# Own tokens and keys transposed by DMAs, and the state pass on two pairs of PSUM banks

## The reference, cut to what matters

```python
xm = rmsnorm(x, norm_w) * (1.0 + sc_x) + sh_x            # modulation from c
parts_x, (qx, kx, vx) = split_heads(xm @ w_in, rotary=True)   # w_in: 1024 x 9216
s_f, s_b = ctx_final_states(kc, vc, lg[0], lg[1])        # from the context tokens
# retention, chunks of 128 positions, 8 heads, k 64 wide and v 128 wide, both directions:
scores = einsum('bhnid,bhnjd->bhnij', qc, kc) * dmask
inner = einsum('bhnij,bhnjv->bhniv', scores, vc)
kv = einsum('bhnjd,hj,bhnjv->bhndv', kc, k_dec, vc)      # each chunk's addition to the state
s = chunk_decay * s + kv                                 # chunk after chunk
cross = einsum('bhnid,hi,bhndv->bhniv', qc, q_dec, s_prev)
y_a = (silu(za) * bg * (dwconv(cg * h) + conv_b)) @ w_a  # the convolution branch
y_b = (silu(zb) * groupnorm(inner + cross)) @ w_b        # the retention branch
x = x + g_x * ((sigmoid(ga) * y_a + sigmoid(gb) * y_b) @ w_out)
out = rmsnorm(x, final_norm_w)
```

## Time and profile before

| | |
|---|---|
| time, median of 3 runs | 910.59 us (909.9 to 910.84) |
| the profiled execution, its own time | 909.72 us |
| its span on the slowest core (core 7) | 908.2 us |
| spans of the eight cores | 898.9 to 908.2 us |
| PE, DVE, ACT, POOL busy over the span | 90%, 49%, 40%, 35% |
| state pass, core 7 | 137.66 to about 251 us |

### The profile page before, as it was taken

One profiled execution on the slowest core, in us unless ns is written; L12 is line 12 of the kernel. 1 busy time (PEld: TensorE's weight loads), 2 busy tenths in 40 slices (PEclk: granted clock), 3 DMA queues, 4 the chain that ended last, 5 costly groups with the idle time before them and its releaser, 6 DMA issues.

```text
span 908.2 us, 14424 instructions; the slowest of 8 cores (898.9 to 908.2 us)
## 1 busy us (share of the span) xinstructions
PE 815.4 (90%) x4656; PEld 394.1 (43%) x4656; DVE 447.4 (49%) x1057; ACT 366.9 (40%) x653; POOL 318.5 (35%) x337
## 2 busy tenths in 40 slices
PE   0179999989975999998989999999999999999995
PEld 0145455545543444344444444444444444444442
DVE  3467515656766755666624424442364511343435
ACT  3499556677556434434323212222122211122122
POOL 0046325454567354444510123202242233233341
PEclk9999999989999899999999999999999999999998
DMA  8987603930074134132451362244006070034233
GB/s 245 292 258 189 158 12 100 179 113 7 10 115 96 32 48 48 33 51 52 71 91 25 64 123 41 53 93 93 1 1 139 27 160 0 23 107 150 72 115 139
DMA packets 49824, 82.33 MB, mean 91 GB/s; under 512 B 29259, under 2 KB 35531, under 8 KB 48086
## 3 DMA queue, kind: packets, MB, share of 16 engines
q1 hardware_dynamic: 44422, 54.14, 21.5%
q0 software_dynamic: 5328, 27.27, 17.0%
HBM read 93.72 MB, written 8.39 MB: 112 GB/s over the span
## 4 chain that ended last, share of the span: by engine, by line
PE 76%; DVE 7%; ACT 7%; DMA 5%; issue 3%; POOL 1%; SPq 1%; DVEq 0%; ACTq 0%; POOLq 0%
PE P L989 51%; PE P L560 12%; PE P L1253 6%; DMA wt<-ada_w 4%; ACT tm L967 2%; DVE vb L1004 2%; PE P L676 2%; PE P L456 1%; DVE tm L815 1%; DVE cm L941 1%; ACT st L892 1%; PE P L620 1%; PE P L933 1%; PE P L934 1%; PE P L801 1%
## 5 line engine op out<-in xcount | busy, mean ns | idle before, releaser
L989 PE MATMUL P<-xmt,vb 128*128 128x512 bf16 x1280 | 283.1, 379 | 2.7 <-DVE wt L1152 1.8
L989 PEld LDWEIGHTS P<-xmt,vb 128*128 128x128 bf16 x1280 | 124.5, 98 | 152.5 <-issue 3.6
L560 PE MATMUL P<-wt,xmt 128*128 128x512 bf16 x688 | 163.0, 389 | 5.7 <-ACT xmt L482 3.4
L989 PE MATMUL P<-xmt,wt 128*128 128x512 bf16 x512 | 118.3, 383 | 1.5 <-ACT tm L967 1.5
L560 PEld LDWEIGHTS P<-wt,xmt 128*128 128x128 bf16 x688 | 65.8, 100 | 84.3 <-issue 15.0
L1155 POOL TENSOR_TENSOR kz<-tm,wt 128x1024 bf16<-128x1024 f32 x16 | 45.7, 2857 | 161.3 <-DVE wt L1152 161.3
L989 PEld LDWEIGHTS P<-xmt,wt 128*128 128x128 bf16 x512 | 49.7, 99 | 59.3 <-issue 4.4
L1232 DVE SCALAR_TENSOR_TENSOR tm<-tm,P 128x512 f32<-128x512 f32 x32 | 22.0, 688 | 87.5 <-PE P L989 87.5
L989 PE MATMUL P<-vb,wt 128*128 128x512 bf16 x256 | 60.0, 387 | 5.5 <-DVE vb L1004 5.5
L1234 POOL TENSOR_TENSOR st<-st,tm 128x512 bf16<-128x512 bf16 x32 | 39.8, 1245 | 65.8 <-DVE tm L1232 65.8
L1108 DVE TENSOR_TENSOR wt<-P,wt 128x512 f32<-128x512 f32 x32 | 22.2, 693 | 80.9 <-ACT wt L1107 60.0
(11 more groups left out here) (163 smaller groups left out, 1109.7 us busy)
## 6 DMA issues: line engine op xcount, KB each, us to landing
kz<-x SPq DMA_DIRECT2D x24, 512.0 KB, 8.1
wt<-x SPq DMA_DIRECT2D x24, 512.0 KB, 4.3
vb<-w_conv POOLq DMA_DIRECT2D x16, 512.0 KB, 7.4
out<-wt SPq DMA_DIRECT2D x15, 512.0 KB, 3.6
st<-ada_w SPq DMA_DIRECT2D x2, 2048.0 KB, 13.9
wt<-ada_w SPq DMA_DIRECT2D x2, 2048.0 KB, 28.6
vb<-w_mix POOLq DMA_DIRECT2D x8, 512.0 KB, 8.7
cm<-rope SPq DMA_DIRECT2D x33, 64.0 KB, 3.2
```

The source lines that it names most:

```text
L560: ins = e.matmul(pf(bank)[:, 0:wid], lhsT=lhs_x(ch, k), rhs=w[:, k, c0_:c0_ + wid], start=(k == 0), stop=(k == 7))
L989: ins = e.matmul(pf(bank), lhsT=lhs(k), rhs=rhs(k), start=(k == 0), stop=(k == 7))
```

## The change

Four things change, all in the state pass or just ahead of it.

- **Own tokens.** `f_tp` is gone for own pairs. A new `f_dtp` lets SP transpose a chunk's scaled rows by one DMA from `xs` straight into `xm`, and `f_aff(pair, True)` modulates them there in place. The DMAs of a pair are issued at the end of the loop's pass in which it was scaled, one pair earlier than its PE transposes stood.
- **Keys.** `w2` has a DMA from SP in place of the PE transposes and ACT's copy; the rotated keys have four buffers in place of two.
- **States.** A chunk's two states go to banks 5 and 6 or to 7 and 0 in turn, its keys to bank 2 or 1. The state update and the copy are split by banks: DVE takes the first bank while ACT takes the second, then they change over.
- **Weights.** `w_q` comes in two parts of 0.5 MB, in the second and third pair, `w_zb` in four, in the fourth to seventh.

```diff
+        def f_dtp(pair):
+            for ch in pair:
+                blk, j = ch["xm"]
+                P.dma("sp", lambda e, ch=ch, blk=blk, j=j: e.dma_start_transpose(out=xm[blk][:, :, j * 128:(j + 1) * 128], in_=ch["xs"][0]),
+                      f"tx{ch['n'] % 4}", reads=[ch["xs"][1]], writes=[f"xm{blk}_{j}"])
...
-            P.op("dve", f_d, reads=["P0", "Amod", "modT"], writes=[n_ + "d" for n_ in names])
-            P.op("act", f_a, reads=["P1", "Amod", "modT"], writes=[n_ + "a" for n_ in names])
+            P.op("dve", f_d, reads=["Amod", "modT"] + (nd if inplace else ["P0"]), writes=nd)
+            P.op("act", f_a, reads=["Amod", "modT"] + (na if inplace else ["P1"]), writes=na)
...
-            proj(2, ch, wk, "wk")
+            kb = 2 if j else 1
+            proj(kb, ch, wk, "wk")
...
+            P.dma("sp", lambda e: e.dma_start_transpose(out=kT[:, n], in_=k_rb[n % 4].rearrange("p h f -> p (h f)")),
+                  f"tk{n % 4}", reads=[f"k_rb{n % 4}"], writes=[f"kT{n}"])
+            kv = (7, 0) if j else (5, 6)
...
+            def stf_half(q):
+                P.op("act", lambda e: e.activation(out=st[0:64, n + 1, q * 512:(q + 1) * 512], in_=pf(kv[q])[0:64, :], func=AF.Copy),
+                     reads=[f"P{kv[q]}"], writes=[f"stf{n + 1}_{q}"])
...
+                P.op("dve", f, reads=[f"P{kv[q]}", f"R{q}", "dec"], writes=[f"R{q}"])
+            for q in range(2):
+                if n > 0:
+                    state_half(q)
+                if n < 15:
+                    stf_half(1 - q)
...
-            if p == 1:
-                wload("wq", wq, wq_d)
-                wload("wzb", wzb, wzb_d)
+            if p in (1, 2):
+                k0 = 4 * (p - 1)
...
             w1(hi)
             if prev:
                 w2(prev)
             if p < 7:
-                f_tp(ownp[p + 1])
-                f_aff(ownp[p + 1])
+                f_aff(ownp[p + 1], True)
             w1(lo_)
             scale2(9 + p + 2)
             w2(hi)
+            if p < 6:
+                f_dtp(ownp[p + 2])
```

More of the change, by code:

```diff
@@ L220, in build_program @@
         own("R", TMP + 4096, 4096, "h")
+        for q in range(2):
+            own(f"R{q}", TMP + 4096 + q * 2048, 2048, "h")
         kc = at(TMP + 8192, [128, 8, 64], BF16)
@@ L223, in build_program @@
         own("kcs", TMP + 8192, 2048)
-        k_rb = [buf(f"k_rb{i}", TMP + 10240 + i * 1024, [128, 8, 64], BF16) for i in range(2)]
+        k_rb = [buf(f"k_rb{i}", TMP + 10240 + i * 1024 if i < 2 else EX + 6144 + (i - 2) * 1024, [128, 8, 64], BF16) for i in range(4)]
         kfb = [buf(f"kfb{i}", TMP + 12288 + i * 2048, [128, 8, 128], BF16) for i in range(2)]
@@ L255, in build_program @@
             own(f"stb{n}", ST + n * 2048, 2048, "h")
+            for q in range(2):
+                own(f"stf{n}_{q}", ST + n * 2048 + q * 1024, 1024, "l")
         mb = at(ST, [128, 4, 4096], BF16)
@@ L267, in build_program @@
             own(f"wv{k}", WB + k * 2048, 4096)
+        for k in (0, 4):
+            own(f"wq{k}", WQ + k * 1024, 4096)
+        for k in range(0, 8, 2):
+            own(f"wzb{k}", WZB + k * 2048, 4096)
         wk = buf("wk", WGB, [128, 8, 512], BF16)
@@ L648, in build_program @@
             scale2(p + 2)
+            if p == 7:
+                f_dtp(ownp[0])
             load2(p + 4)
@@ L719, in build_program @@
         scale2(10)
+        f_dtp(ownp[1])
         rope2(10)
@@ L800, in f_kv, with state_half, f @@
                 for h in range(8):
-                    ins = e.matmul(pf(5 + h // 4)[:, (h % 4) * 128:(h % 4 + 1) * 128], lhsT=kfb[j][:, h, :],
+                    ins = e.matmul(pf(kv[h // 4])[:, (h % 4) * 128:(h % 4 + 1) * 128], lhsT=kfb[j][:, h, :],
                                    rhs=vb[:, n, h * 128:(h + 1) * 128], start=True, stop=True)
                 return ins
[L804 to L811, removed]
+            P.op("pe", f_kv, reads=[f"kfb{j}", f"v{n}"], writes=[f"P{b}" for b in kv])
+            def stf_half(q):
+                P.op("act", lambda e: e.activation(out=st[0:64, n + 1, q * 512:(q + 1) * 512], in_=pf(kv[q])[0:64, :], func=AF.Copy),
+                     reads=[f"P{kv[q]}"], writes=[f"stf{n + 1}_{q}"])
+            def state_half(q):
+                def f(e):
                     ins = None
-                    for h in range(8):
-                        pk_ = pf(5 + h // 4)[:, (h % 4) * 128:(h % 4 + 1) * 128]
+                    for h in range(4 * q, 4 * q + 4):
+                        pk_ = pf(kv[q])[:, (h % 4) * 128:(h % 4 + 1) * 128]
                         ins = e.scalar_tensor_tensor(out=RF[64:128, h, :], in0=RF[64:128, h, :], scalar=dch[64:128, 8 + h:9 + h],
@@ L817, in f_state @@
                     return ins
-                P.op("dve", f_state, reads=["P5", "P6", "R", "dec"], writes=["R"])
+                P.op("dve", f, reads=[f"P{kv[q]}", f"R{q}", "dec"], writes=[f"R{q}"])
+            for q in range(2):
+                if n > 0:
+                    state_half(q)
+                if n < 15:
+                    stf_half(1 - q)
+            if n > 0:
                 put_stb(n - 1)
```

31 lines of the change are left out of this document (15 added, 16 removed).

## The result

The changed kernel takes **897.94 us** (median of four runs, 897.22 to 903.56) against 910.72 for the kernel before on the same chip: ratio 0.9878, 95% interval 0.9861 to 0.9896, so 1.2% faster. The forecast was 890.0, own range 885 to 893: the sign and most of the mechanism came, 8 us of the gain did not. The time lies outside that range, and inside 885 to 902, which was drawn to hold rivals (1) and (3) as well. The profiled execution took 897.38 us, its slowest core 895.7.

The account below looks back on a forecast made before the run. PE was taken to set the state pass's pace, so work and waits leaving its stream count. Slowest span 887.5 - 0.9 + 1.1 = 887.7, against 908.2; 889.2 for the profiled execution, 890 us as median, range 885 to 893.

Parts of the forecast that it names:

- rival (1): State pass: x rows come late behind transposes and weights, one or two stalls, 895 to 901, say 898 us; chance 0.17.
- rival (3): State pass: DVE's modulation from SBUF and POOL's products block each other, 0.4 to 1.5 six times, say 895 us; chance 0.12.
- PE's stream: First key projection to last state matmuls: 91.2 us of PE work remains, against 113.0 on core 7 and 108.0 on core 4.
- The 0.9 ahead: Ahead of the state pass: the eighth own pair's transposes leave PE's gapless work, another 0.9 us off.
- The state update: State pass: with two pairs of banks and halves crossing over, PE's wait for DVE's update costs nothing.
- The query wait: End of the state pass: PE waits 1.2 us at the first query transposes, against 0.16 before.
- +1.1: End of the state pass: the amount added to the sum for the new wait of 1.2 us against 0.16.
- The weights' stall: State pass: with weights in 0.5 MB parts, x arrives free by 1 us and the stall of 192 us goes.
- The modulation unchanged: State pass: modulating in place from SBUF takes as long as from PSUM, 1.3 us (DVE) and 1.8 (ACT) a pair.
- The cover: State pass pairs of 11.24 us: ACT, DVE and POOL work fits; own transposes landing within 4.3 us are free.
- The landing of 4.4: State pass: own-token transposes land in 4.4 us, the largest measured, costing 0; bounds 3.0 and 8.6.
- The key transposes at nothing: State pass: key transposes by DMA have 16 chunks' time and cost nothing.

Follow-up runs that it names:

- e9: Changed kernel with keys transposed by PE again, one pair of state banks, and POOL's small operations behind the first products: 891.9 to 893.72 us, ratio 0.9813.
- e5: Changed kernel with keys transposed by PE again, own tokens still by DMA, one pair of state banks: 892.95 to 895.01 us, ratio 0.9823.
- e12: Changed kernel with own-token and key transposes back on PE, one pair of state banks; weights in parts and bank split stay: 898.89 to 900.14 us, ratio 0.9887.
- e4: Changed kernel with own tokens transposed by PE again, keys still by DMA, one pair of state banks: 896.22 to 897.92 us, ratio 0.9858.
- e11: e9 with 40 transposes of the identity added on PE before 44 us, where PE waits anyhow: 892.72 to 894.77 us, ratio 0.9825.

## Why the prediction was right in sign and 8 us short

*PE's stream* held: 5.34 and 0.61 everywhere, pairs of 11.25 where nothing waits, 100.5 for the pass with DMA relieved. *The 0.9 ahead* held as work: from the sum over the other half's keys to the first start-state matmul 30.1 us against 31.0, on every core. It did not bring the pass forward (first start-state matmul at 134.0 in the mean, 134.1 before), since that stretch began 0.8 later in this execution. That looks like chance: in the nine other kernels with the same early transposes this matmul comes at 133.2 to 133.8 in the mean, in the four with own tokens on PE at 134.1 to 134.5.

*The state update* at nothing held; the reason was half right, since the split suffices. *The query wait* held: 1.45 for 1.2. But its +1.1 was taken against core 7's 0.16 and added to a sum for core 4. There the row below stood behind the last gap before the change, 5.30 for 16 gate matmuls that take 3.62 without it, so that nothing had to wait; this went with the gap, and the stretch is 5.52 for 5.58.

```profile
245.81 5.30 PE L989 MATMUL P<-xmt,wt 128*128 128x512 bf16 x16
```

*The weights' stall* went as said: rival (1) did not come, and but for one square on core 4 (0.55) ACT waits for no x rows in the pass.

*The modulation unchanged* is the first step that failed. I had the mechanism as rival (3) and gave it 0.12 because no row showed it. That was no evidence: before, this instruction read PSUM, so no row could. On core 0 the waits it made, in four pairs and not in six, bring the first key projection to the last state matmuls to 94.2 us for 91.2: 0.7 for each of the four, within the rival's 0.4 to 1.5. That the modulation grew by just two products was luck, since a third of it is the cast's.

*The cover* is the second. I counted PE, ACT, DVE and POOL, and took single landings for the transposes, but never added up what a pair asks of DMA. It could be read: the row of q1 above, of e9, has one transpose of 128x1024 at 57.0% of 2.40 us, 1.4 us of all sixteen engines (the retention of the kernel before has such transposes, at 56.9% in the same view), and the earlier trace rows have 0.92 over two pairs with weights and x alone. The landing of 4.4 became 3.1 to 9.2 on core 4. *The key transposes at nothing* failed with it: nobody waits for them, but beside them the own ones are late, and without them (e5) no engine waits for an own one. They save PE 3.7 us, and still the kernel with them is 4 to 5 slower, in a share not known because chunk 12's meeting moved.

*What the sum left out*: the retention as unchanged. Core 4 against the sum: 0.8 ahead of the pass, 5.0 in it (96.2 for 91.2; 3.0 as on core 0 and 2.0 for late transposes), 1.2 less between its end and the query transposes, 3.4 in retention: 8.0, from 887.7 to 895.7. That the time lies between what rivals (3) and (1) gave, 895 and 898, is luck in part: the pass alone misses by what (3) has at its middle, and the rest comes from a stage that no rival names. Of the retention's 2.2 in the mean, chunk 12's meeting with the instruction packets is 2.1; chunk 8's, now missed, gives 1.1 back; the first two chunks cost some 1.3 more.

By parts: weights in parts 3.3 us, the split by banks (with the four key buffers) some 7. From there the two kinds of transposes don't add up. Own tokens by DMA alone bring some 6 (e12 to e5), keys by DMA alone some 3 (e12 to e4), and both together nothing over e12 that can be told from none.

## What to carry to other kernels

Count DMA as an engine: what a period asks of it in microseconds of all queues, before work is moved there, since a transpose that nobody waits for can still delay the one that somebody does. Two moves to the same engine are to be priced together: here each gained alone, and both together nothing that can be told from none. A wait that the trace cannot show, because the instruction has other operands today, is not thereby unlikely. After a change of instruction counts, look for moved delays in stages that the change doesn't touch.

## What the hardware showed that was not expected

- With a 16 KB packet of PE's instruction stream in its flight, a DMA transpose of 256 KB landed mostly in 4 to 5.8 us in place of 3.0; which transposes it meets moves with PE's instruction count (e9 and e11).
- DVE and POOL shut each other out in the other direction too. At the first chunk of retention POOL's 8-wide power takes 2.65 us when DVE adds two f32 tiles from SBUF at that moment; in the kernel before, where POOL began first, it took 1.67. POOL and then DVE, core 6 of the changed kernel:

```profile
245.05 2.65 POOL L980 TENSOR_TENSOR cm<-cm 128x8 f32<-128x8 f32 x1 [0.45 <-DVE cm L978]
```

```profile
244.94 1.22 DVE L913 TENSOR_TENSOR tm<-tm,st 64x1024 f32<-64x1024 f32 x1
```

- DMA moved some 190 GB/s while a transpose alone kept the engines full (e9, the flight above: 0.26 MB in 1.4 us of all sixteen), and 391 over two microseconds of e5's pass (core 1, from 167 us). The Trainium skill (Advanced Engine Details and Errata, section DMA Advanced Topics) calls transposes as fast as other DMAs, at 350 to 400 GB/s; these runs show about half, and the measurement decides.
